# Gated feed-forward: two panels as seven block products, finished by additions from SBUF

## The reference

```python
h = rmsnorm(x, norm) * (1 + scale) + shift
gate, value = split(h @ ffn_w_in)          # 1024 x 5632: 2816 gate columns, 2816 value columns
x = x + g * ((silu(gate) * value) @ ffn_w_out)   # 2816 x 1024
```

## Time and profile before

| what | value |
|---|---|
| median of 3 runs | 2556.62 us (2556.59 to 2557.61) |
| profiled execution | 2558.0 us |
| its span, first to last instruction | 2556.2 us |
| PE busy | 2527.6 us, 99% |
| PE weight loads | 2044.6 us, 80% |
| DVE busy | 1144.6 us, 45% |
| ACT busy | 675.3 us, 26% |
| POOL busy | 1323.7 us, 52% |
| chain that ended last | PE 96%, DVE 2%, ACT 1% |

### The profile page before, as it was taken

One profiled execution on the slowest core, in us unless ns is written; L12 is line 12 of the kernel. 1 busy time (PEld: TensorE's weight loads), 2 busy tenths in 40 slices (PEclk: granted clock), 3 DMA queues, 4 the chain that ended last, 5 costly groups with the idle time before them and its releaser, 6 DMA issues.

```text
span 2556.2 us, 35249 instructions
## 1 busy us (share of the span) xinstructions
PE 2527.6 (99%) x14535; PEld 2044.6 (80%) x14535; DVE 1144.6 (45%) x1972; ACT 675.3 (26%) x1343; POOL 1323.7 (52%) x562
## 2 busy tenths in 40 slices
PE   8999999999999999999999999999999999999998
PEld 6787778888887877788888767888888888888887
DVE  4445565666534446656665344322224134422224
ACT  5245451111123454511101443200002233200002
POOL 5543236665665423465556733565555522565555
PEclk9999999999999999999999999999999999999999
DMA  8221034655332211346652211323222211223221
GB/s 267 83 61 50 26 110 146 197 191 183 106 116 83 60 34 50 116 148 197 193 183 86 86 34 51 111 97 98 98 99 83 83 50 34 83 99 98 98 98 66
DMA packets 220448, 265.36 MB, mean 104 GB/s; under 512 B 19236, under 2 KB 192892, under 8 KB 220188
## 3 DMA queue, kind: packets, MB, share of 16 engines
q1 hardware_dynamic: 217628, 256.72, 31.3%
q10 hardware_dynamic: 2688, 6.76, 0.8%
HBM read 258.74 MB, written 4.72 MB: 103 GB/s over the span
## 4 chain that ended last, share of the span: by engine, by line
PE 96%; DVE 2%; ACT 1%; DMA 0%; ACTq 0%; issue 0%; DVEq 0%; PEldq 0%; PEld 0%
PE PS L1027 10%; PE PS L1031 10%; PE PS L1030 10%; PE PS L1776 5%; PE PS L1779 5%; PE PS L1780 5%; PE PS L975 5%; PE PS L980 4%; PE PS L979 4%; PE PS L1295 1%; PE PS L1299 1%; PE PS L1298 1%; DVE PROJR L3093 1%; PE PS L2072 1%; PE PS L1907 1%; PE PS L2130 1%
## 5 line engine op out<-in xcount | busy, mean ns | idle before, releaser
L871 POOL TENSOR_SCALAR WH<-RAW 128x2048 fp32r<-128x2048 f32 x178 | 341.6, 1919 | 1035.9 <-issue 909.2
L873 POOL TENSOR_TENSOR WL<-RAW,WH 128x2048 fp32r<-128x2048 f32 x178 | 823.2, 4625 | 14.9
L1027 PE MATMUL PS<-Hh,WL 128*128 128x512 f32 x1152 | 448.6, 389 | 0.0
L1030 PE MATMUL PS<-Hl,WH 128*128 128x512 f32 x1152 | 448.2, 389 | 0.0
L1031 PE MATMUL PS<-Hh,WH 128*128 128x512 f32 x1152 | 448.1, 389 | 0.0
L2812 DVE SCALAR_TENSOR_TENSOR X<-PS,X 128x512 f32<-128x512 f32 x304 | 207.0, 688 | 185.6 <-PE PS L1780 123.3
L1031 PEld LDWEIGHTS PS<-Hh,WH 128*128 128x128 f32 x1152 | 216.2, 188 | 45.1
L1027 PEld LDWEIGHTS PS<-Hh,WL 128*128 128x128 f32 x1152 | 216.2, 188 | 45.0 <-issue 0.4
L1030 PEld LDWEIGHTS PS<-Hl,WH 128*128 128x128 f32 x1152 | 216.2, 188 | 44.7
L3210 DVE TENSOR_TENSOR PS<-SQ,PS 128x512 f32<-128x512 f32 x44 | 30.6, 696 | 427.2 <-PE PS L1031 427.2
L1776 PE MATMUL PS<-U,WL 128*128 128x512 f32 x512 | 200.1, 391 | 0.0
(11 more groups left out here) (585 smaller groups left out, 4660.3 us busy)
## 6 DMA issues: line engine op xcount, KB each, us to landing
RAW<-in_w_ff SPq DMA_DIRECT2D x64, 1024.0 KB, 5.5
PROJ<-in_ada_w SPq DMA_DIRECT2D x48, 1024.0 KB, 8.3
RAW<-in_ffn_w_in SPq DMA_DIRECT2D x44, 1024.0 KB, 5.1
RAW<-in_ffn_w_out SPq DMA_DIRECT2D x22, 1024.0 KB, 4.9
RAW<-in_w_in SPq DMA_DIRECT2D x20, 1024.0 KB, 5.3
RAW<-in_w_out SPq DMA_DIRECT2D x8, 1024.0 KB, 5.0
RAW<-in_a_w_in SPq DMA_DIRECT2D x6, 1024.0 KB, 5.2
RAW<-in_b_w_in SPq DMA_DIRECT2D x12, 512.0 KB, 5.0
```

The costliest lines, as they stand in the source:

```text
L871: pool.tensor_scalar(WH[b][:, :], RAW[b][:, :], 1.0, 1.0, ALU.mult, ALU.mult).then_inc(s.split_hi, 1)
L873: pool.tensor_tensor(WL[b][:, :], RAW[b][:, :], WH[b][:, :].bitcast(F32), ALU.subtract).then_inc(s.split_done, 1)
L1027: ins = mm(bank, WL[b][:, col:col + P], Hh[:, k, :], start=k == 0, stop=False)
L1030: mm(bank, WH[b][:, col:col + P], Hl[:, k, :], start=False, stop=False)
```

## The change

In chunks 2 to 10 (`FAST_FROM = 2`) the gate panel and the value panel (`FAST = (0, 1)`) are computed as a 2x2 block product in seven products instead of eight. The blocks are: the 1024 contraction in two halves of 4 k-tiles, the 256 weight columns in two halves of 128, the 512 tokens in two halves of 256. One product is 4 k-tiles x 3 matmuls of 256 columns.

- Products need four sums of weight blocks and four sums of blocks of normalized tiles. The latter are made once per feed-forward (`normed_sums`, `normed_sums_low`); for that ScalarE also writes the normalized tiles whole (`full=True`).
- The weight sums are made by VectorE from `RAW` (`weight_sums`, eight operations of 128x512 per chunk; those of the gate panel between additions of `hidden`, those of the value panel between the first four residual additions). ScalarE makes their high halves (`sums_high`), GpSimd the low halves in four pieces (`split_fast`).
- The high halves of the fast weight panels are made by ScalarE (`panel_high`) instead of GpSimd; GpSimd makes the low halves of the three quarters that are used, in pieces of 512. All other panels of these feed-forwards are split by GpSimd with the subtraction in four pieces (`split_pieces`).
- Inside a fast panel ScalarE copies the first product into another bank (`copy_first`), on which TensorE goes on accumulating, and two partial results to SBUF (`copies`); VectorE finishes three of the four quarters with additions from these copies (`combine_first`, `combine`). TensorE waits for `copy_first` before the third product and for `combine_first` before the fifth.
- Gate and value panels now take three banks each (0 to 2, 3 to 5), and the down panel the banks 6, 7, 0, 1, 2, 6, 7, 1 (`DOWN_BANKS`, `DOWN_FREE`).
- `DB` holds gate sums, so the load of the distances is issued after the first feed-forward.

The diff, cut to its core (SP's queue is unchanged):

```diff
+DOWN_BANKS = 6, 7, 0, 1, 2, 6, 7, 1
+DOWN_FREE = -2, -1, 0, 0, 0, 1, 2, 4
...
+            def split_fast(at, z, n):
+                b = at % 2
+                pool.wait_ge(fa.sums_hi, fa.sums_hi_0 + (4 * (n // FAST_PANELS + 1) + n + 1))
+                apart(pool)
+                for q in range(4):
+                    c = slice(S * q, S * q + S)
+                    ins = pool.tensor_tensor(w_sums_lo(z)[:, c], w_sums(z)[:, c], w_sums_hi(z)[:, c].bitcast(F32), ALU.subtract)
+                ins.then_inc(s.part_lo, 1)
+                pool.wait_ge(s.panels_begun, at + 2)
+                pool.wait_ge(s.split_hi, at + 1)
+                first = lambda x: x[:, 0:1024].rearrange("p (k i c) -> p k i c", k=4, i=2)[:, :, 0, :]
+                pool.tensor_tensor(first(WL[b]), first(RAW[b]), first(WH[b]).bitcast(F32), ALU.subtract)
+                for q in range(2, 4):
+                    c = slice(S * q, S * q + S)
+                    ins = pool.tensor_tensor(WL[b][:, c], RAW[b][:, c], WH[b][:, c].bitcast(F32), ALU.subtract)
+                ins.then_inc(s.split_done, 1)
...
+                    product(a, weight(0, 0), normed(0, 0), start=True, begun=True).then_inc(fa.products, 1)
+                    pe.wait_ge(fa.sums, fa.sums_0 + (FAST_PANELS * 4 * w + 9 * (w + 1)))
+                    product(d, weight_sum(0), normed_sum(0), start=True).then_inc(fa.products, 1)
+                    pe.wait_ge(fa.copied, fa.copied_0 + (n * 3 + 1))
+                    product(b22, weight_sum(1), normed_sum(1)).then_inc(fa.products, 1)
+                    product(a, weight(0, 1), normed(1, 0))
+                    pe.wait_ge(fa.combined, fa.combined_0 + (n * 4 + 1))
+                    product(b22, weight_sum(2), normed_sum(2)).then_inc(fa.products, 1)
+                    product(c12, weight_sum(3), normed(1, 1), start=True).then_inc(fa.products, 1)
+                    product(c21, weight(1, 1), normed_sum(3), start=True).then_inc(s.g_tile, 2)
...
+                def up(c, b, at, fast):
+                    for z in range(2):
+                        if fast and z in FAST:
+                            if z:
+                                pe.wait_ge(s.ulo, c * 2 + (u0 + 2))
+                            else:
+                                pe.wait_ge(s.f_evac, c * 8 + (f0 + BANKS - 16 + 5))
+                            up_fast(z, (b + z) % 2, at + z, (c - FAST_FROM) * len(FAST) + (FAST_PANELS * w + FAST.index(z)))
+                        elif z:
+                            hidden_t((b + 1) % 2, at + 1, 3, s.ulo, c * 2 + u0)
+                        else:
+                            hidden_t(b, at, 0, s.r32, c * 2 + (u0 - 66))
...
+                def down(c, e, b, at, silus):
                     pe.wait_ge(s.ulo, c * 2 + (u0 + 4))
-                    panel_t(b, at, [([(k * D + f * P, k) for k in range(2)], P) for f in range(KT)],
-                            c * 8 + f0, 4, tile_sem=s.f_tile, evac=s.f_evac, act=lambda k, lo: U[:, e, k, lo, :])
+                    begin(at)
+                    for i in range(KT):
+                        bank = PS[:, DOWN_BANKS[i], :]
+                        if i == 2:
+                            pe.wait_ge(s.r32, silus)
+                        pe.wait_ge(s.f_evac, c * 8 + (f0 + BANKS + DOWN_FREE[i]))
+                        for k in range(2):
+                            col = k * D + i * P
+                            ins = mm(bank, WL[b][:, col:col + P], U[:, e, k, 0, :], start=k == 0, stop=False)
+                            if i == 0 and k == 0:
+                                ins.then_inc(s.panels_begun, 1)
+                            mm(bank, WH[b][:, col:col + P], U[:, e, k, 1, :], start=False, stop=False)
+                            ins = mm(bank, WH[b][:, col:col + P], U[:, e, k, 0, :], start=False, stop=k == 1)
+                        ins.then_inc(s.f_tile, 1)
...
+                def copy_first(z, c):
+                    n = number(z, c)
+                    act.wait_ge(fa.products, fa.products_0 + (n * 5 + 1))
+                    if z == 0:
+                        act.wait_ge(s.f_evac, c * 8 + (f0 + BANKS - 8))
+                    f(PS[:, 3 * z + 1, 0:256], PS[:, 3 * z, 0:256], ACT.Copy).then_inc(fa.copied, 1)
+                def copies(z, c):
+                    n = number(z, c)
+                    act.wait_ge(fa.products, fa.products_0 + (n * 5 + 2))
+                    f(p5_copy(z), PS[:, 3 * z + 2, 0:256], ACT.Copy).then_inc(fa.copied, 1)
+                    act.wait_ge(fa.products, fa.products_0 + (n * 5 + 4))
+                    f(p167_copy(z), PS[:, 3 * z + 1, 0:256], ACT.Copy).then_inc(fa.copied, 1)
+                def panel_high(z, c, b):
+                    act.wait_ge(s.panels_begun, c * 3 + (first + 1 + z))
+                    f(WH[b][:, :], RAW[b][:, :], ACT.Copy).then_inc(s.split_hi, 1)
+                def sums_high(z, c):
+                    if z in FAST:
+                        act.wait_ge(fa.sums, fa.sums_0 + ((c - FAST_FROM) * len(FAST) * 4 + ((FAST_PANELS * w + FAST.index(z) + 1) * 4 + 9 * (w + 1))))
+                        f(w_sums_hi(z), w_sums(z), ACT.Copy).then_inc(fa.sums_hi, 1)
+                def chunk(c, e, fast, ahead, normed=False):
+                    b0 = (first + e) % 2
+                    gate_fast, value_fast = (fast and z in FAST for z in range(2))
+                    if value_fast:
+                        panel_high(1, c, b0)
+                    if gate_fast:
+                        copy_first(0, c)
+                        copies(0, c)
+                        act.wait_ge(fa.combined, fa.combined_0 + (number(0, c) * 4 + 4))
+                    if value_fast:
+                        copy_first(1, c)
+                    halves = range(2) if gate_fast else range(1)
+                    for j in range(2):
+                        act.wait_ge(s.g_tile, c * 4 + (g0 + j + 1))
+                        for h in halves:
+                            src = quarter(0, True, j, h) if gate_fast else PS[:, j, :]
+                            dst = SQ[:, j, 256 * h:256 * h + 256] if gate_fast else SQ[:, j, :]
+                            ins = f(dst, src, ACT.Silu)
+                        ins.then_inc(s.r32, 1)
+                    if normed:
+                        for x in range(4):
+                            act.wait_ge(fa.sums, fa.sums_0 + ((FAST_PANELS * 4 + 9) * w + x + 2))
+                            f(h_sums_hi(x), h_sums(x), ACT.Copy).then_inc(fa.sums_hi, 1)
+                    if value_fast:
+                        copies(1, c)
+                    if ahead:
+                        sums_high(0, c + 1)
+                        panel_high(0, c + 1, b0)
+                    for j in range(2):
+                        if value_fast:
+                            act.wait_ge(s.u_in, c * 2 + (u0 + 2))
+                            for h in range(2):
+                                ins = f(U[:, e, j, 0, 256 * h:256 * h + 256], quarter(1, True, j, h), ACT.Copy)
+                            if j:
+                                ins.then_inc(s.uhi, 2)
+                        else:
+                            act.wait_ge(s.u_in, c * 2 + (u0 + j + 1))
+                            f(U[:, e, j, 0, :], PS[:, 3 + j, :], ACT.Copy).then_inc(s.uhi, 1)
+                    if ahead:
+                        sums_high(1, c + 1)
+                chunk(0, 0, False, False, normed=True)
+                chunk(1, 1, False, True)
+                with act.Fori(0, (FF2_CHUNKS - 3) // 2) as c2:
                     for e in range(2):
-                        gated(g0, u0, c2 * 2 + e, e)
-                gated(g0, u0, FF2_CHUNKS - 1, 0)
+                        chunk(c2 * 2 + (2 + e), e, True, True)
+                chunk(FF2_CHUNKS - 1, 0, True, False)
 
...
+                def combine_first(z, c):
+                    n = number(z, c)
+                    v.wait_ge(fa.products, fa.products_0 + (n * 5 + 3))
+                    v.wait_ge(fa.copied, fa.copied_0 + (n * 3 + 2))
+                    v.tensor_tensor(p156(z), PS[:, 3 * z + 1, 0:256], p5_copy(z), ALU.add).then_inc(fa.combined, 1)
+                def combine(z, c):
+                    n = number(z, c)
+                    c21, b22, c12 = PS[:, 3 * z, 256:512], PS[:, 3 * z + 1, 0:256], PS[:, 3 * z + 2, 256:512]
+                    v.wait_ge(fa.copied, fa.copied_0 + (n * 3 + 3))
+                    v.tensor_tensor(b22, p5_copy(z), b22, ALU.add).then_inc(fa.combined, 1)
+                    v.wait_ge(fa.products, fa.products_0 + (n * 5 + 5))
+                    v.wait_ge(fa.combined, fa.combined_0 + (n * 4 + 1))
+                    v.tensor_tensor(c12, p156(z), c12, ALU.add).then_inc(fa.combined, 1)
+                    v.wait_ge(s.g_tile, c * 4 + (g0 + 2 * z + 2))
+                    v.tensor_tensor(c21, p167_copy(z), c21, ALU.add).then_inc(fa.combined, 1)
...
+                def weight_sums(z, c, at, loaded, steps):
+                    if z not in FAST:
```

(56 more changed lines are left out.)

## The result

The changed kernel takes 2599.0 us (median of four runs; 2594.5 to 2601.0) against 2556.8 for the kernel before: a ratio of 1.016, 95% interval 1.015 to 1.018, so 42 us slower. The forecast was 2602.

What follows compares the result with a forecast made beforehand. TensorE, busy 99% of the span, bounds the kernel. Each feed-forward adds 4.1 + 8 x 2.48 - 1.0 = 22.9 us, two 45.8; 2556.6 + 45.8 = 2602 us, range 2587 to 2626.

Steps and rivals of the forecast that it cites:

- The sum: Both feed-forwards together: 22.9 us longer each from entry, eight longer periods and last chunk, 45.8 us in all.
- TensorE's share: Fast gate and value panels: 84 narrow matmuls 0.120 us apart, a chunk's TensorE work 31.05 us, 1.62 less.
- Rival D: Fast panels: narrow matmuls don't keep 0.120 us, each showing its weight load of 0.19; 2739 us, chance 0.02.
- The chain: Once per chunk through GpSimd, load, VectorE, TensorE and ScalarE: seven steps of 35.15 us against TensorE's 31.05.
- The three waits: TensorE before value panel's fifth product 2.0 us, last down tile 1.5, gate panel's third product 0.6.
- Weight sums at the port: VectorE's weight sums: each waits out GpSimd's current piece (0 to 1.28 us), takes 0.55, delays GpSimd some 0.45.
- rival C: GpSimd's pieces keep VectorE's weight sums out for a whole run: period 39.1 us, total 2666, chance 0.13.
- Rival B: No waits between GpSimd and VectorE: period 33.0 us, total 2566, chance 0.13.
- New operations: Prices of added operations: ScalarE's 2048-column copy 1.9 us, VectorE's 256-column operation 0.345, GpSimd's 512-column piece 1.28.
- Ends: Per feed-forward: entry with normalization and first sums 4.1 us more, last chunk without next sums 1.0 less.
- Rival A: The round per chunk closes under 31.05 us, so TensorE alone counts: 2530 us, chance 0.17.
- link 4: TensorE in the value panel from the fifth product: 0.3 us, then three products of 4.3; 4.6 in all.

Runs made afterwards that it cites:

- e7: Changed kernel with GpSimd splitting the value panel before its sums, VectorE's residuals 0 to 5 before value sums, ScalarE's sum copy inside the next chunk: 2532.9 us.
- e3: Changed kernel with VectorE adding the first four down tiles ahead of all four value sums instead of alternating them: 2592.2 us.
- e6: Changed kernel with GpSimd making the value panel's low half ahead of the low halves of its weight sums: 2568.5 us.
- e4: Changed kernel with each value sum taking one operand from a down tile in PSUM instead of SBUF, contents wrong: 2572.4 us.
- e2: Changed kernel with one more GpSimd piece of 1.28 us in each fast panel: 2638.7 us.
- e1: Changed kernel without GpSimd's low halves of the weight sums, all matmuls kept: 2549.0 us.
- e5: Changed kernel with only the gate panel by seven products, the value panel made as before the change: 2544.9 us.
- e9: Reordered kernel e7 with one more GpSimd piece of 1.28 us in each fast panel, as in e2: 2563.1 us.
- e10: Changed kernel loading only half of each gate panel's bytes, except in each feed-forward's first chunk: 2575.1 us.
- e8: Reordered kernel e7 with GpSimd's old order put back, low halves of the value sums before the value panel's: 2646.1 us.

## Why the prediction held, step by step

The forecast was 2602, with 0.77 for slower; it came out at 2599 through the mechanism it named. That the total is off by only 3 us is in part luck (see The sum).

- **TensorE's share** was right: 0.120 us, 31.05 us of work a chunk (e7 runs at 31.08). Rival D, and the rule from the Trainium skill (TensorE: Matmul & The Clock Gate, Back-to-back issue gap) that stood beside it, are out: the trace gives 0.53 of the wide spacing, not 0.75.
- **The chain**, link by link, foreseen and read off the rows above: (1) GpSimd's seven pieces 9.2, 8.97 (1807.01 to 1815.98); (2) load 5.25, 5.32 (to 1821.30); (3) two gate sums and the first addition 2.8, 2.71 (to 1824.01); (4) three products 4.6, 4.46 (to 1828.47); (5) end of the panel to the first residual 5.15, 4.88 (to 1833.35); (6) residuals and value sums 6.2, 6.38 (last sum 1839.05 + 0.68); (7) copy 1.95, 1.95. Sum 35.15, 34.67. No link is off by more than 0.3; (1), (3), (4) and (5) were too dear, (2) and (6) too cheap, and the 0.48 that is left makes 7.7 us over 16 periods.
- **The three waits** were placed rightly: 2.0, 1.5 and 0.6 foreseen, 2.0, 1.3 and 0.3 measured. But e3 shows that their lengths are not prices. Each is where the one chain's excess surfaces, and it can be moved without being lost.
- **Weight sums at the port.** Foreseen: a waiting sum gets in after the piece under way, takes 0.55 more and holds GpSimd up by 0.45. The second gate sum came at 1.70, the second value sum at 1.12, GpSimd's pieces beside them at 1.52 for 1.28 alone:

```profile
L3469 DVE TENSOR_TENSOR DB<-RAW 128x512 f32<-128x512 f32 x18 | 30.6, 1699 | 0.0
...
L3469 DVE TENSOR_TENSOR ATT<-RAW 128x512 f32<-128x512 f32 x18 | 20.1, 1119 | 0.0
...
L942 POOL TENSOR_TENSOR WL<-RAW,WH 128x512 fp32r<-128x512 f32 x72 | 107.6, 1516 | 0.0
```

  Not every sum waited: three of the eight in the chunk of the timeline took 0.68 or 0.69 us. The rows exclude rival C (37 or more, with sums kept out of a whole run of pieces). The Trainium skill (SBUF — State Buffer, SBUF: two separate sides) has this as a lock that is held for a whole instruction; the trace agrees, in e6 most plainly. Rival B, no waits of that kind, is excluded by e4: without the value sums' share alone the period is 33.4, so they cost.
- **New operations.** The 2048-column copy was put at 1.9 and took 1.92; the 256-column addition ran at 0.33 to 0.34 from start to start where I took 0.345.
- **Ends.** From the first normalization of one feed-forward to the next layer's, before and then after:

```profile
1607.37 0.94 DVE L2798 SCALAR_TENSOR_TENSOR PS<-X,GN,PS 128x256 f32<-128x256 f32 x2 [0.87 <-PE PS L1121]
...
1972.42 0.94 DVE L2798 SCALAR_TENSOR_TENSOR PS<-X,GN,PS 128x256 f32<-128x256 f32 x2 [0.87 <-PE PS L1121]
```

```profile
1606.95 0.94 DVE L3026 SCALAR_TENSOR_TENSOR PS<-X,GN,PS 128x256 f32<-128x256 f32 x2 [0.87 <-PE PS L1209]
...
1991.36 0.94 DVE L3026 SCALAR_TENSOR_TENSOR PS<-X,GN,PS 128x256 f32<-128x256 f32 x2 [0.87 <-PE PS L1209]
```

  365.05 and 384.41: +19.4. Seven of its eight periods are 2.00 longer and one, with a fall of the clock, 3.16; that leaves 2.2 for entry and last chunk, foreseen 3.1 (4.1 - 1.0). The second feed-forward has the remaining 17.6 of the profile's 36.5 (the start was 0.4 earlier): 16.0 in periods, 1.6 at its ends.
- **The sum** fits better than its parts, by luck. Foreseen 45.8, less 7.7 for the periods, less 2.4 for the ends, gives 35.7; the median shows 42.2. Most of the gap is a term that the prediction lacks: the clock, 1.2 us in the profile and 4.5 more in the median (last section). Another 1.2 is the kernel before, whose profiled run (2558.0) lies that much above its median. So chain and ends were too dear by some 10 us, and the missing terms made up for most of it.
- **Rival A** was judged by its distance, 4.1 us of chain. That distance was about right (34.67 - 31.05 = 3.6), but I took the chain as a property of the work. It is one of the order of three queues: e6 closes part of it and e7 all, with the same operations.

## What to carry to other kernels

When a change makes TensorE's work shorter and gives the difference to other engines, don't add up their busy times: follow one buffer all the way round (split, reload, sums, product, split) and compare the sum of the links with TensorE's work for the same round. If the round is longer, waits on TensorE show where it surfaces, not what to repair; shorten the round itself, first by taking work for later out from ahead of the operation that frees the buffer. If you let one engine make something later, look at every queue that waits for it in order: the same two moves in VectorE's and ScalarE's queues gave -66 us together with the new order on GpSimd, and +47 with the old one. And when two runs differ in granted clock, compare what a change costs in chunks at full clock: e2's total says 40 us, its undisturbed periods 23.

## What I had not expected of the hardware

- **TensorE's clock fell after some of its waits of 1.7 us.** In the changed kernel, the first steady chunk: TensorE resumes after 1.73 us idle, and a microsecond later gets half the clock (the matmul, then stretches of 1 us, the granted clock ahead of the DMA share):

```profile
1684.26 0.39 PE L1941 MATMUL PS<-PROJR,ATTR 128*128 128x256 f32 x1 [1.73 <-DVE PTS L3443]
...
1685.00:1686.00 1.00, 1.00 (x8) 1.00 (x8) 0.97 (x2) 0.00 (x0) 0.01 (x1) 0.68 0.00 0
1686.00:1687.00 1.00, 1.00 (x7) 1.00 (x7) 0.49 (x2) 0.63 (x2) 0.00 (x0) 0.50 0.64 110
1688.00:1689.00 1.00, 1.00 (x8) 1.00 (x7) 0.00 (x0) 0.55 (x1) 0.27 (x1) 0.61 1.07 376
```

  The granted clock is 0.50, the lower level of 1.2 GHz, from 1685.3 to 1688.6; matmuls start 0.21 apart instead of 0.12, right in link 4, and this period is 35.83 us instead of 34.67: 1.16 us dearer. In e2, where nine of sixteen periods hold such a stretch, it is some 21/9 = 2.3 for each, waits that grow with it included. It happens after some of these waits and not after others: in the profile once, with a mean clock of 0.999; the runs at 2599.0, 2599.0 and 2601.0 us have 0.996 or 0.997. An estimate of what that costs: from 0.999 to 0.9965 is 2597 x 0.0025 x 2 = 13 us at the lower level, four more such stretches of 3.3 us, at 1.16 each 4.6 us, near the 4.5 of the median. The other kernels bear this out. e4, which keeps the wait before the fifth product, has runs of 2568.7 and 2570.0 at 0.999, and 2574.9 and 2575.3 at 0.996 and 0.997. In e1, e5, e6, e7, e9 and e10, where TensorE's waits in these feed-forwards are at most 1.2 us long (in e6 one of 1.7), no run is under 0.999, and the runs of each lie within 1.2 us of each other. That the waits bring the fall is inferred from this; no run changes their length alone. The Trainium skill (TensorE: Matmul & The Clock Gate, What's actually happening) names these two levels and a fall after idleness. The trace agrees on the levels; its fall begins a microsecond after the wait has ended, and stays out after most waits of the same length.
- **In e8 it comes about once a chunk.** The rows of e8 above show it after 3.14 us idle; the mean clock of 0.988 is 63 us at the lower level, some 3.5 for each of 18 chunks. Yet its period was foreseen as 37.7 without any of this and came out at 37.35. A reason would be that matmuls that ran slower would have waited for VectorE before the fifth product anyway: in the chunk shown 0.30 us of idle time are left of that wait, of some 3 expected. That is argued, not shown, as no period of e8 is without such a stretch to compare with.
- **Half a panel is not half a load.** 1 MB lands after 5.1 us and 0.5 MB after 3.5: a term that doesn't shrink with the bytes, by a straight line through the two an estimated 1.9 us.
